# Two feed-forward up stages in which six of 22 gate and value pairs are computed as seven half-size products

## The reference, cut to what matters

```
def conv_ffn(xn, w_up, conv_w, conv_b, w_down):
    h = causal_dwconv(xn @ w_up, conv_w) + conv_b
    gate, val = h[..., :FFN_DIM], h[..., FFN_DIM:]
    return (jax.nn.silu(gate) * val) @ w_down
```

## Time and profile before

| | us |
|---|---|
| median of 3 runs | 1757.93 (1757.25 to 1758.06) |
| profiled execution | 1757.99 |
| its span, first to last instruction | 1756.3 |
| TensorE busy | 1734.1 |
| VectorE busy | 1178.9 |
| ScalarE busy | 880.3 |

### The profile page before, as it was taken

How to read it: one execution, slowest core, us unless ns; L and a number is a source line. 1 busy time by engine, 2 the same in 40 slices (tenths; PEclk the granted TensorE clock), 3 DMA queues, 4 the chain that set the end, 5 groups by cost and what they waited for, 6 DMA issues and landing times.

```text
span 1756.3 us, 26012 instructions
## 1 busy us (share of the span) xinstructions
PE 1734.1 (99%) x9344; PEld 1371.2 (78%) x9344; DVE 1178.9 (67%) x1964; ACT 880.3 (50%) x1413; POOL 51.5 (3%) x85
## 2 busy tenths in 40 slices
PE   9999999999999999999999999999999999999998
PEld 6777777778888888788887788888888766678987
DVE  6788888567777733467776677777433567677875
ACT  6666666444444422368777444444332456654442
POOL 2000000000000000000000000000000000101100
PEclk9999999999999999999999999999999999999999
DMA  5522221133223332233332332332421311336631
GB/s 186 182 78 73 72 70 52 49 120 94 89 92 96 107 107 85 77 115 106 104 110 66 108 90 91 95 96 69 143 86 63 111 36 61 102 101 137 157 109 66
DMA packets 49857, 169.14 MB, mean 96 GB/s; under 512 B 6273, under 2 KB 8596, under 8 KB 49776
## 3 DMA queue, kind: packets, MB, share of 16 engines
q1 hardware_dynamic: 42864, 149.83, 26.4%
q0 software_dynamic: 6480, 18.14, 4.3%
q10 hardware_dynamic: 432, 0.07, 0.0%
HBM read 161.39 MB, written 6.63 MB: 96 GB/s over the span
## 4 chain that ended last, share of the span: by engine, by line
PE 89%; DVE 4%; ACT 3%; issue 2%; DMA 1%; POOL 0%; SPq 0%; DVEq 0%; ACTq 0%
PE acc L750 21%; PE acc L752 20%; PE acc L751 20%; PE acc L776 9%; PE pbc L1135 1%; PE pbc L1210 1%; ACT wsplit L1388 1%; DMA wraw<-w 1%; PE pa L750 1%; PE pa L752 1%; PE pa L751 1%; PE acc L1295 1%; PE acc L1296 1%; PE acc L1297 1%; PE pa L1198 1%
## 5 line engine op out<-in xcount | busy, mean ns | idle before, releaser
L750 PE MATMUL acc<-xhi,wsplit 128*128 128x512 f32 x1088 | 443.2, 407 | 1.0 <-DVE at_vs L2456 1.0
L1388 ACT ACTIVATE wsplit<-wraw 128x1024 fp32r<-128x1024 f32 (+1 forms) x229 | 251.9, 1102 | 377.0 <-PE acc L752 360.1
L752 PE MATMUL acc<-xhi,wsplit 128*128 128x512 f32 x1088 | 431.6, 397 | 0.0
L751 PE MATMUL acc<-xlo,wsplit 128*128 128x512 f32 x1088 | 431.4, 396 | 0.0
L2010 DVE TENSOR_TENSOR wsplit<-wraw,wsplit 128x1024 fp32r<-128x1024 f32 (+1 forms) x226 | 288.7, 1279 | 134.6 <-ACT wsplit L1388 133.7
L750 PEld LDWEIGHTS acc<-xhi,wsplit 128*128 128x128 f32 x1088 | 205.0, 188 | 62.9 <-issue 13.8
L752 PEld LDWEIGHTS acc<-xhi,wsplit 128*128 128x128 f32 x1088 | 204.9, 188 | 49.6
L751 PEld LDWEIGHTS acc<-xlo,wsplit 128*128 128x128 f32 x1088 | 205.4, 189 | 46.4 <-issue 1.4
L776 PE MATMUL acc<-xhi,wsplit 128*128 128x512 f32 x464 | 158.2, 413 | 0.1
L751 PE MATMUL acc<-hid_lo,wsplit 128*128 128x512 f32 x352 | 139.6, 396 | 0.0
L752 PE MATMUL acc<-hid_hi,wsplit 128*128 128x512 f32 x352 | 139.6, 396 | 0.0
(11 more groups left out here) (487 smaller groups left out, 2918.0 us busy)
## 6 DMA issues: line engine op xcount, KB each, us to landing
wraw<-w SPq DMA_DIRECT2D x213, 512.0 KB, 3.6
wraw<-w SPq DMA_DIRECT2D x32, 704.0 KB, 4.1
wraw<-w SPq DMA_DIRECT2D x21, 256.0 KB, 3.5
bias_dram<-ext_dram POOLq DMA_DIRECT2D x1, 4096.0 KB, 21.1
bias<-bias_dram POOLq DMA_DIRECT2D x16, 256.0 KB, 3.2
at_ks<-at_ks SPq DMA_DIRECT2D x16, 256.0 KB, 2.9
wraw<-w POOLq DMA_DIRECT2D x14, 256.0 KB, 5.3
crow<-row_dram POOLq DMA_DIRECT2D x8, 256.0 KB, 3.7
```

The costliest lines, as they stand in the source:

```text
L750: mm(out, whi[:, k, :], a[:, x_at + k, :], start=(k == first), stop=False)
L751: mm(out, whi[:, k, :], b[:, x_at + k, :], start=False, stop=False)
L752: m = mm(out, wlo[:, k, :], a[:, x_at + k, :], start=False, stop=(k == last))
L1388: A(split(s, i, j, 0), raw(s, j), ACT.Copy).then_inc(w_hi_ready, 1)
```

## The change

In both up stages f = 0 and 1 stay as they were. From f = 2 on each pair has its own waits, written out without loops. The pairs f = 4, 7, 10, 13, 16 and 19 are computed as seven half-size products in the order a11, s2, a12, s1, s3, s4, a22, with the gate's two input halves and the value's two as the four weight quarters; the other 14 stay two whole tiles, gate in a bank of pa and value in pb. For the products four turned inputs (xb) are made from x_raw: eight copies on ScalarE after row 0, four turns and four low parts on VectorE and four high parts on ScalarE within f = 2 and 3. s1 and s3 are each a load and an adding load of GpSimd's queue, s2 and s4 sums on VectorE. All weights go through the ring of six slots; gate tiles have one raw buffer, value tiles one. Rows 0 to 5 of hid are split at once, rows 6 and 7 after f = 20, the others after f = 21, between the casts of the down stage's first weights, and its first body waits for them row by row. Renamed semaphores (merge_dve to block_dve and the like) and their shifted counts are left out here.

```diff
+UP_FIRST = 2
+UP_BLOCKS = (4, 7, 10, 13, 16, 19)
+UP_FORMS = ("a11", "s2", "a12", "s1", "s3", "s4", "a22")
+UP_KEPT = 6
...
+    places = 4 * (KF - UP_FIRST) + 4 * len(UP_BLOCKS)
+    spread = UP_BLOCKS[:(-places) % RING // 2]
+
+    def width(f, name):
+        if f not in UP_BLOCKS:
+            return 2
+        return 1 if name != "a22" else 4 if f in spread else 2
+
...
+    after = {u: [] for u in units + ["old2", "old3"]}
+    for f, name in units:
+        top = slots[f, name] + (1 if f in UP_BLOCKS else 2) - 1 - RING
+        after[owner[top] if top >= 0 else "old2" if top < 2 - RING else "old3"].append((f, name))
+    return units, slots, after
...
+                    for f in range(UP_FIRST, KF):
+                        if f == UP_FIRST:
+                            sp.wait_ge(w_lo_ready, s.number(0, 0) + 1)
+                        elif f - 1 in UP_BLOCKS:
+                            sp.wait_ge(ev("block_dve"), UP_DVE[layer, "low", (f - 1, "a12")])
+                            sp.wait_ge(ev("block_dve"), UP_DVE[layer, "s4", f - 1])
+                        else:
+                            sp.wait_ge(ev("block_dve"), UP_DVE[layer, "low", (f - 1, "gate")])
+                        load_gate(f)
+                        if f not in UP_BLOCKS:
...
+                                sp.wait_ge(ev("block_dve"), UP_DVE[layer, "low", (before[-1], "value")])
...
+                            load_value(f)
+                        if f + 2 in UP_BLOCKS:
+                            k = UP_BLOCKS.index(f + 2)
+                            if k:
+                                sp.wait_ge(ev("block_dve"), UP_DVE[layer, "low", (UP_BLOCKS[k - 1], "a22")])
+                            else:
+                                sp.wait_ge(w_lo_ready, s.number(0, 3) + 1)
+                            load_bases(f + 2)
+                    sp.wait_ge(ev("block_dve"), UP_DVE[layer, "low", UNITS[-1]])
+                    sp.wait_ge(ev("block_dve"), UP_DVE[layer, "ev", UP_BLOCKS[-1], 1])
...
+            def up_sums(layer):
+                s = st[f"up{layer}"]
+                for f in UP_BLOCKS:
+                    pool.wait_ge(raw_landed[2], bases_landed_at(layer, f))
+                    pool.dma_start(unit_raw((f, "s1")), w8[s.src + 2 * f + 1, :, 512:1024], accum_op=ALU.add
+                                   ).then_inc(ev("sums_landed0"), 16)
+                    pool.dma_start(unit_raw((f, "s3")), w8[s.src + 2 * f + 1, :, 0:512], accum_op=ALU.add
...
+                def half(i, j, rows):
+                    pe.wait_ge(w_lo_ready, s.number(i, j) + 1)
+                    if j % 2 == 0:
+                        pe.wait_ge(acc_free, s.number(i, j) - 2)
+                    for k0, k1 in rows:
+                        if k1 - k0 == 1:
+                            pe.wait_ge(ev("hid_lo_ready"), KF * layer + KH * (j % 2) + k1)
...
+                for j in range(s.n):
+                    half(0, j, [(k, k + 1) for k in range(KH)] if j < 2 else [(0, KH)])
...
+                u = (f, ("gate", "value")[g])
...
+                pe.wait_ge(ev("block_dve"), UP_DVE[layer, "low", u])
+                if before:
+                    pe.wait_ge(ev("block_dve"), UP_DVE[layer, "ev", before[-1], g])
...
+                at = UP_BLOCKS.index(f)
+                pe.wait_ge(ev("block_dve"), UP_DVE[layer, "low", u])
+                if at == 0:
+                    if name == "a11":
+                        pe.wait_ge(acc_free, st[f"up{layer}"].number(0, 3) + 1)
+                    if name in ("s2", "s1", "s3", "a22"):
+                        pe.wait_ge(ev("block_dve"), UP_DVE[layer, "turn_low", {"s1": 0, "s2": 1, "s3": 2, "a22": 3}[name]])
+                elif name == "a11":
+                    pe.wait_ge(ev("block_act"), UP_ACT[layer, "p", UP_BLOCKS[at - 1]])
+                else:
+                    step = {"s2": "c21", "a12": "c11", "s1": "w", "s3": "v", "s4": "c12", "a22": "c21"}[name]
+                    pe.wait_ge(ev("block_dve"), UP_DVE[layer, step, UP_BLOCKS[at - 1]])
+                if name == "a22":
+                    pe.wait_ge(ev("block_dve"), UP_DVE[layer, "u", f])
...
+                    if j == 1:
+                        for k in range(KD):
+                            A(x_raw[:, k, :], h[:, k, :], ACT.Copy, scale=xgain[:, k, :]).then_inc(ev("block_act"), 1)
+                    if j == 2:
+                        casts_after("old2")
+                casts_after("old3")
...
+                casts_after("old3")
+                d = st[f"down{layer}"]
+                for f in range(UP_FIRST, KF):
+                    if f in UP_BLOCKS:
+                        act.wait_ge(ev("form_used"), unit_used(layer, (f, "a11")))
+                        if f != UP_BLOCKS[0]:
+                            act.wait_ge(ev("block_dve"), UP_DVE[layer, "c11", UP_BLOCKS[UP_BLOCKS.index(f) - 1]])
+                        A(unit_p, bank_1, ACT.Copy).then_inc(ev("block_act"), 1)
+                        for name in UP_FORMS[:-1]:
+                            casts_after((f, name))
+                        newest(f, 0)
+                        casts_after((f, "a22"))
+                        newest(f, 1)
+                        gate_silu(f)
+                    else:
+                        casts_after((f, "gate"))
+                        if f == KF - 1:
+                            act.wait_ge(ev("form_used"), unit_used(layer, (f, "gate")))
+                            cast(d, 0, 0)
+                        newest(f, 0)
+                        if f == UP_FIRST:
+                            turn_hi(0)
+                            turn_hi(1)
+                        casts_after((f, "value"))
+                        newest(f, 1)
+                        gate_silu(f)
+                        if f == UP_FIRST:
+                            turn_hi(2)
+                            turn_hi(3)
+                    if f < UP_KEPT:
+                        row_hi(f)
+                    if f == KF - 2:
+                        for k in range(UP_KEPT, 8):
+                            row_hi(k)
+                    if f == KF - 1:
+                        for k in range(8, KH):
+                            row_hi(k)
+                        act.wait_ge(ev("form_used"), unit_used(layer, (f, "value")))
+                        cast(d, 0, 1)
+                        for k in range(KH, KF):
+                            row_hi(k)
...
+                    if j == 2:
+                        lows_after("old2")
+                lows_after("old3")
...
+                def block(f):
+                    lows_after((f, "a11"))
+                    dve.wait_ge(ev("block_act"), UP_ACT[layer, "p", f])
+                    used(f, "s2")
+                    tt_(unit_u, unit_p, bank_64, ALU.subtract).then_inc(steps, 1)
+                    lows_after((f, "s2"))
+                    used(f, "a12")
+                    taken(f, 0)
+                    tt_(tmp[:, 0, 0:HALF], bank_2, unit_p, ALU.add).then_inc(steps, 1)
+                    lows_after((f, "a12"))
+                    used(f, "s1")
+                    dve.wait_ge(steps, UP_DVE[layer, "u", f])
+                    tt_(unit_w, bank_5, unit_u, ALU.add).then_inc(steps, 1)
+                    lows_after((f, "s1"))
+                    used(f, "s3")
+                    taken(f, 1)
+                    dve.wait_ge(steps, UP_DVE[layer, "w", f])
+                    tt_(tmp[:, 1, HALF:S], bank_7, unit_w, ALU.subtract).then_inc(steps, 1)
+                    tt_(unit_v, bank_7, unit_u, ALU.subtract).then_inc(steps, 1)
+                    lows_after((f, "s3"))
+                    used(f, "s4")
+                    tt_(tmp[:, 0, HALF:S], bank_3, unit_w, ALU.add).then_inc(steps, 1)
+                    dve.wait_ge(steps, UP_DVE[layer, "c12", f])
+                    tt_(tmp[:, 0, :], tmp[:, 0, :], rstd[:], ALU.mult).then_inc(steps, 1)
+                    lows_after((f, "s4"))
+                    used(f, "a22")
+                    dve.wait_ge(steps, UP_DVE[layer, "v", f])
+                    tt_(tmp[:, 1, 0:HALF], bank_64, unit_v, ALU.add).then_inc(steps, 1)
+                    dve.wait_ge(steps, UP_DVE[layer, "c21", f])
+                    tt_(tmp[:, 1, :], tmp[:, 1, :], rstd[:], ALU.mult).then_inc(steps, 1)
+                    lows_after((f, "a22"))
+                    conv(f, 0)
+                    conv(f, 1)
+
+                def pair(f):
+                    used(f, "gate")
+                    taken(f, 0)
+                    tt_(tmp[:, 0, :], pa[:, 0, :], rstd[:], ALU.mult).then_inc(steps, 1)
+                    lows_after((f, "gate"))
+                    if f == KF - 1:
+                        low(d, 0, 0)
+                    conv(f, 0)
+                    if f + 1 in UP_BLOCKS:
+                        sum_high(f + 1)
+                    if f == UP_FIRST:
+                        turn(0, x11r, x12r, ALU.subtract)
+                        turn(1, xb_raw[0][:], x22r, ALU.add)
```

(73 more changed lines are left out.)

470 lines of the change are left out of this document (330 added, 140 removed).

## The result

The changed kernel takes 1780.05 us (1778.16 to 1780.4) against 1757.99 (1757.25 to 1758.49) for the kernel before: ratio 1.0124, 95% interval 1.0106 to 1.0141. It is 22 us slower; 1784 was forecast, with 1768 to 1797 as the range.

A forecast was written before the change was run, and what follows sets the result against it. TensorE was taken to set the time of both up stages. Stalls of 2 x (19.25 + 0.3) + 2.5 = 41.6 us, less 15.2 saved, gave +26.4 and so 1784 us, range 1768 to 1797.

The forecast's parts named there:

- Saving: Up stages: seven half-size products for two whole tiles save 1.27 us a block, 15.2 us over 12 blocks.
- g2: Gate of f = 2: TensorE stalls 3.6 us a layer for VectorE's low part, behind copies, newest, cast and conv.
- v2 and v3's load: Value of f = 2 stalls 1.5 us behind row 1's chain; v3's load goes out after low v2, landing 3.6 later.
- First s2: Block 4's second product stalls 8.8 us a layer for turn_low 1, late in VectorE's queue.
- s3: Block 4's product s3 stalls 1.1 us a layer for turn_low 2, behind conv and row of f = 3.
- Late gates and g6: Behind blocks 4 and 7, gates cast after s4: g5 stalls 2.3 us, g8 1.25; g6, loaded late, 0.7, each layer.
- The end: Start of the down stages: late rows and third down weight stall 0.7 + 0.3 us, then 0.7 + 0.8; 2.5 together.
- Blocks 10 to 19 at nothing: Rest of the up stage from block 10 on: no waits, with 1.8 us of cover at the nearest place.
- The clock: TensorE's clock may fall after the 3.6 and 8.8 us gaps: 0.3 us a layer added, bounds 0 and 3.
- The sum: Whole kernel: 41.6 us of stalls, less 15.2 saved, is +26.4 us, so 1784 us.
- TensorE's busy time: Profile of the changed kernel: TensorE busy about 15 us less.

The follow-up runs named there:

- repaired run without turns: Changed kernel with plain input quarters in place of turned inputs, v2 split early and spare slots at value tiles: 1746.29 us, 0.994 of the kernel before.
- last run: Changed kernel, blocks and turns where they were, with x_raw copies split, v2 split early and spare slots at value tiles: 1760.62 us, 1.0018 of the kernel before.
- ninth run: Against the run with five later blocks and four repairs, only ScalarE's x_raw copies and turned inputs' high parts moved: 1748.86 us, 0.9945 of the kernel before.
- tenth run: Same ScalarE moves as the ninth run, but six blocks a layer from f = 5: 1754.78 us, 0.9982 of the kernel before.

## Why the prediction was right, point by point

**Saving.** 15.2 us was forecast from the earlier trace rows. The repaired run without turns gives 1757.55 - 1746.29 = 11.3 us, plus its waits of 0.98, 1.62 and 0.3: 14.2, and its four executions spread over 5 us. Its page shows TensorE busy 1717.5 us, 16.6 less than before. That fits the rows of the changed kernel: a block without waits takes 9.85 us (525.85 to 535.70) and not 9.97, and two pairs of whole tiles 22.49, so a block saves 1.39 us. The forecast was right, and low by 1.4 us in all.

**g2.** Copies, newest, conv, cast, low part, in that order: right, shown by moving the copies. 3.6 was forecast, 2.8 measured. The walk took 0.89 us between the two conv steps from the earlier trace rows, and they took 0.79; row 0's high part, behind two such convs, came 17.13 us after the start of the stage and not 17.58, and the conv of T2 was shorter too.

**v2 and v3's load.** Right: the load went out when low v2 ended and landed 3.5 us later. v2's wait of 1.5 stands as such only where g2 runs at full clock and doesn't come late.

**First s2.** The mechanism was right and the size, 8.8 for 7.1 and 7.4, was too large. Counted from the start of the stage, turn_low 1 ended 2.5 us sooner than forecast (58.6 for 61.1), and TensorE was at s2 0.6 sooner. Seven conv steps shorter by 0.1, and waits of 0.70 at two rows where rows in the loop showed 0.92, make up 1.1 of the 2.5, and shorter waits for ScalarE behind the turns 0.5. The forecast also said that about 6 us would stay against a start without stalls, by VectorE's work alone. The last run gave 5.5 and 6.3, but that is luck in part: there VectorE started on g2's low part 4 us sooner than the forecast had it (21.5 us after the start of the stage, not 25.6), and was idle 4.4 us where that reading has it idle for none.

**s3.** Wrong by 1.1 us a layer: turn_low 2 ended at about 430.0, 5 us after s2 began at 424.97, and with the clock at half for a time the products before s3 took longer than that (5.6 us, to 430.60). The fall paid for this wait, as the text had for part of it.

**Late gates and g6.** Right in place, and 30% to 50% smaller at g5. 1.15 us is what the wider a22 costs by itself, at g8 here and at g5 in the run without turned inputs; the forecast had 1.05 more at g5 for VectorE's late work, and 0.45 and nothing came. Moving the spare slots removed all of them.

**The end.** 2.5 us forecast, 2.6 measured (0.98 and 1.62), the same in every run with late rows.

**Blocks 10 to 19 at nothing.** Right in all runs: no wait at any block from the third on.

**The clock.** 0.3 us a layer was forecast; about 0.5 and 1.35 in layer 0 and 1.9 in layer 1 were measured. Both waits of s2 were followed by a fall. I had counted on s3's wait to absorb 1.1 of each, and that wait did go, but more than 0.3 was left. With s3's wait the forecast had 1.4 us a layer for the two together, against 1.85 and 1.9. By the rule of the Trainium skill (TensorE: Matmul & The Clock Gate, "HAM oscillation — how this bites in real kernels") each long enough wait is paid for again; the trace agrees for both waits of s2 (clock 0.63 and 0.52). The two waits at g2, of 2.8 us, were paid for once (0.70) and once not (1.00).

**The sum.** Waits of 30.1 and 4.8 for the clock came where 41.6 were forecast: 6.7 too much. In the changed stages 26.4 us were forecast as lost and 20.2 measured. The 2.2 us that lie outside of these stages brought the measured time nearer to 1784; that part of the agreement is luck.

**TensorE's busy time.** The text said about 15 us less, and the page shows 6.9 less. The lower clock accounts for 4.8 of the difference; the rest is not explained.

What I had not seen is how to repair it. That VectorE's work alone causes the wait at the start was my reading when I moved the blocks. The three runs that moved blocks or turns first (one pair later; five blocks; six blocks) ran into waits elsewhere, and my numbers for them were off by 11 to 20 us, always too fast. For five blocks the ninth run shows that waits of the two engines for each other were the cause.

## What to carry to other kernels

A cheaper product is worth its price only where the engines that feed it have room at that very place: here the steady part had it and the first 30 us had not. One set-up in each stage, 9.8 us of work on VectorE with its copies and casts on ScalarE, cost 24.6 us in the place it had, more than 12 cheaper blocks gave; with the same set-up spread out, five blocks a layer paid. Set-up work goes into the idle gaps of each queue in pieces, behind whatever the other engine waits for. A step that waits never goes in front of a cast that doesn't. When a wait is taken away, look at the next thing that the late engine owes: with one bank for the gates it was the scaling out of that bank.

## What the runs showed of the hardware that was not expected

Two dependent VectorE steps (L2418 and L2421, the conv) start 0.89 us apart in the old kernel's loop, and 0.78 apart in its last body, which stands behind the loop (604.77 and 605.55), as in the changed kernel, which has no loop there (0.79). What makes the difference wasn't tried.

Waits of the same length at g2 (2.8 us as steps) were followed by the lower clock in one layer and not in the other. It is so in the changed kernel (granted clock over the next 5.6 us 0.70, then 1.00) and in the run with each block one pair later (0.70, 1.00), while the run with the spare slots elsewhere shows the fall in both layers (0.70, 0.70). Even the waits of 2.1 us at the first s2 of the tenth run were followed by a fall once (0.62 over the next 4 us) and once not (1.00). What decides it is open.
